# Routed expert rows: scaled when they leave PSUM, read back once at the end, added by VectorE and GpSimd

## The reference, cut to what matters

```python
h = modulate(rmsnorm(x, norm2), sh2, sc2)
x = x + g2 * hier_moe(h, ...)

def hier_moe(h, ...):
    # top-1 of 4 groups, then the top-2 of its 8 experts: two (expert, weight) pairs a token
    combine = ...                       # (tokens, groups, experts), two entries a token
    for g in range(4):
        a = einsum('td,edf->tef', t, w1[g]); b = einsum('td,edf->tef', t, w3[g])
        hid = silu(a) * b * combine[:, g, :, None]
        out = out + einsum('tef,efd->td', hid, w2[g])
```

## Time and profile before

| | |
|---|---|
| Median of 3 runs | 665.71 us (665.36 to 668.84) |
| The profiled execution | 666.92 us |
| Its span, first to last instruction | 665.1 us |
| TensorE matmul busy | 604.8 us, 91% of the span |
| VectorE busy | 304.1 us, 46% |
| GpSimd busy | 93.7 us, 14% |
| Moved from and to HBM | 165.36 MB read, 15.74 MB written |
| Mean granted TensorE clock | 0.973 of full speed |

### The profile page before, as it was taken

The page is one execution under the profiler, slowest core; times in us unless marked ns, Lnnn a source line. Parts: engine busy times, 40 slices in busy tenths (PEclk is TensorE's granted clock), DMA queues, the critical chain, the costliest instruction groups (busy, mean ns, idle before and its releaser), DMA issues.

```text
span 665.1 us, 7868 instructions
## 1 busy us (share of the span) xinstructions
PE 604.8 (91%) x3008; PEld 361.3 (54%) x3008; DVE 304.1 (46%) x606; ACT 168.9 (25%) x368; POOL 93.7 (14%) x136
## 2 busy tenths in 40 slices
PE   2699797889999999999999989999999987989785
PEld 0444585667767677774588834454444433434233
DVE  0229989375454444119525384332232322245167
ACT  3024031034444425343202301232222211112010
POOL 2022241037600000000000020211111111100000
PEclk9999899879999999999999999999999998999899
DMA  8994945923180303051456674799999999999963
GB/s 313 398 356 176 337 146 181 378 99 126 61 320 1 127 1 127 1 191 61 183 242 272 214 312 150 299 410 422 419 421 419 420 419 419 423 418 422 387 260 127
DMA packets 41498, 173.85 MB, mean 261 GB/s; under 512 B 6268, under 2 KB 6332, under 8 KB 28660
## 3 DMA queue, kind: packets, MB, share of 16 engines
q1 hardware_dynamic: 34128, 159.40, 60.6%
q0 software_dynamic: 5744, 12.84, 5.4%
q10 hardware_dynamic: 1588, 1.10, 0.5%
HBM read 165.36 MB, written 15.74 MB: 272 GB/s over the span
## 4 chain that ended last, share of the span: by engine, by line
PE 62%; DMA 14%; DVE 8%; SPq 6%; issue 6%; POOL 3%; ACTq 1%; ACT 1%; DVEq 0%; POOLq 0%
PE bank L917 11%; PE bank L642 6%; PE bank L644 6%; PE bank L643 6%; PE bank L949 5%; DMA late<-in_w_dram 4%; DMA arena<-in_w_dram 4%; PE bank L732 4%; SPq L520 3%; POOL ss L1877 3%; DMA qkg<-in_k_norm_dram 2%; PE bank L822 2%; DMA late<-in_w_in_dram 2%; PE bank L932 2%; PE bank L823 2%
## 5 line engine op out<-in xcount | busy, mean ns | idle before, releaser
L917 PE MATMUL bank<-arena,hT 128*64 128x512 f32 x352 | 86.2, 631 | 8.5 <-DMA arena<-in_w_dram 7.5
L642 PE MATMUL bank<-hT_high,w_in_parts 128*128 128x512 f32 x160 | 67.0, 419 | 3.3 <-DVE w_in_parts L1330 3.3
L644 PE MATMUL bank<-hT_high,w_in_parts 128*128 128x512 f32 x160 | 63.7, 398 | 0.0
L643 PE MATMUL bank<-hT_low,w_in_parts 128*128 128x512 f32 x160 | 63.6, 398 | 0.0
L917 PEld LDWEIGHTS bank<-arena,hT 128*64 128x64 f32 x352 | 24.5, 142 | 50.0 <-issue 40.9
L1199 ACT COPY probs<-bank 128x512 f32<-128x512 f32 x32 | 18.7, 586 | 121.3 <-PE bank L917 121.3
L1606 DVE TENSOR_SCALAR hT<-bank,ab 128x128 f32<-128x128 f32 x64 | 21.8, 403 | 50.1 <-PE bank L902 50.1
L917 PE MATMUL bank<-late,hT 128*64 128x512 f32 x160 | 39.0, 632 | 3.6 <-DMA late<-in_w_dram 3.6
L949 PE MATMUL bank<-arena,g1b 128*64 128x512 f32 x176 | 39.7, 593 | 2.2 <-DVE g1b L1621 2.2
L932 PEld LDWEIGHTS bank<-fold,probs 128*128 128x128 f32 x256 | 32.7, 197 | 16.0 <-issue 11.4
L1364 DVE TENSOR_REDUCE st<-bank 128x2 f32<-128x256 f32 (+3 forms) x16 | 13.2, 824 | 57.9 <-PE bank L668 57.8
(11 more groups left out here) (285 smaller groups left out, 1007.0 us busy)
## 6 DMA issues: line engine op xcount, KB each, us to landing
arena<-in_w_dram SPq DMA_DIRECT2D x66, 1024.0 KB, 23.0
late<-in_w_dram SPq DMA_DIRECT2D x30, 1024.0 KB, 24.2
late<-in_w_ada_dram SPq DMA_DIRECT2D x6, 2048.0 KB, 12.7
arena<-in_w_ada_dram SPq DMA_DIRECT2D x5, 2048.0 KB, 9.6
arena<-in_w_in_dram SPq DMA_DIRECT2D x4, 2048.0 KB, 16.8
late<-in_w_in_dram SPq DMA_DIRECT2D x4, 2048.0 KB, 11.2
y_scratch<-route POOLq DMA_DIRECT2D x1, 4096.0 KB, 14.9
late<-in_w_out_dram SPq DMA_DIRECT2D x2, 2048.0 KB, 7.6
```

The costliest lines, as they stand in the source:

```text
L642: mm(bank[:, b, :], wH[:, b, k, :], hH[:, k, :], start=k == 0, stop=False)
L643: mm(bank[:, b, :], wH[:, b, k, :], hL[:, k, :], start=False, stop=False)
L644: last = mm(bank[:, b, :], wL[:, b, k, :], hH[:, k, :], start=False, stop=k == 7)
L917: last = mm(bank[r, 2 + n % 2, :].rearrange("p (w f) -> p w f", w=2), xgT[n // 2 % 2][:, k, SLOTS * (n % 2):SLOTS * (n % 2 + 1)], w13[s][: ...
```

## The change

It does five things.

1. The weights of all 32 experts are spread to slots, not those of the last four. `combine_weights` runs before `one_hot(1, ...)`, on `[128, 4 x 32]` instead of `[128, 4 x 4]`. `weight_sums` gives all sixteen pairs four matmuls each: pairs 0 and 1 between the warming matmuls after `slot_sums(0)`, the others inside expert 1's gate_up.
2. Every `drain_y` multiplies by the slot's weight (a scalar per partition) as well as by `g2b`.
3. The stored rows are then added without a weight: `tensor_tensor` add, tiles 0 and 1 on VectorE (`BY_DVE = 2`), tiles 2 and 3 on GpSimd, each first for j = 0 and then for j = 1. VectorE's first two adds come after `hidden(31)`, its other two after the low parts of the last pair. All wait for all four readback DMAs, on one semaphore.
4. The readback waits, besides the scatters, for the landing of the last expert's w2. The ring loads go w1/w3 of e + 1 and e + 2, then w2 of e and e + 1.
5. Two warming matmuls of 256 columns stand ahead of gate_up(30), ahead of gate_up(31) and after it, and the one-hot spreading matrix is built at expert 29 instead of 31.

```diff
+BY_DVE = 2
...
             def load_pair(e):
-                for j in range(2):
-                    sp.wait_ge(ab_done, e + j + 1 - RING)
-                    load13(e + j, (e + j) % RING)
+                for n in range(e + 1, min(e + 3, E)):
+                    sp.wait_ge(ab_done, n + 1 - RING)
+                    load13(n, n % RING)
                 sp.wait_ge(y_done, e // 2 + 1 - RING // 2)
-                for j in range(2):
-                    load2(e + j, (e + j) % RING)
+                for n in range(e, e + 2):
+                    load2(n, n % RING)
...
-            sp.wait_ge(ab_done, 2)
-            load13(RING + 1, 1)
-            sp.wait_ge(y_done, 1)
-            load2(RING, 0)
-            load2(RING + 1, 1)
-            for e in range(RING + 2, E, 2):
+            for e in range(RING, E, 2):
                 load_pair(e)
...
             for i in range(3):
                 sp.wait_ge(y_stored[i], 16 * len(range(i, STORED, 3)))
-            rows_of(y_d, yg_loaded)
+            sp.wait_ge(w2_loaded[(E - 1) % RING], 16 * ((E - 1) // RING + 1))
+            for t in range(TT):
+                sp.dma_start(yg[:, t], y_d[2 * P * t:2 * P * (t + 1), :].rearrange("(p j) d -> p j d", j=2)
+                             ).then_inc(yg_loaded, 16)
...
+            def weight_sums(g, q):
+                e = 2 * (q - IDX_GROUPS[g][0])
+                for t in range(TT):
+                    lhs = place[g][t][:, e:e + 2, :].rearrange("p e s -> p (e s)")
+                    last = mm(bank[:, 7, W0 + 6 * q:W0 + 6 * q + 6], lhs,
+                              cparts[:, t, 2 * q:2 * q + 2, :].rearrange("p e c -> p (e c)"),
+                              start=t == 0, stop=t == TT - 1)
+                return last
...
             slot_sums(0)
-            keep_warm(7, 5)
+            keep_warm(5, 5)
+            pe.wait_ge(weights_ready, 1)
+            for q in IDX_GROUPS[0]:
+                weight_sums(0, q)
+            keep_warm(2, 5)
...
                     fold_halves(n - 1)
+                if n >= E - 2:
+                    keep_warm(2, 0, 0, CH // 2)
                 gate_up(n)
                 if n % 2 == 0 and n >= 2:
                     down(n - 2)
+                if n == E - 1:
+                    keep_warm(2, 0, 0, CH // 2)
...
-                    last = v.tensor_tensor(ysb[q % 3][:, w], bank[:, 6 + h, :], g2b[:, w], ALU.mult)
+                    last = v.scalar_tensor_tensor(out=ysb[q % 3][:, w], in0=bank[:, 6 + h, :], scalar=cws[:, q:q + 1],
+                                                  in1=g2b[:, w], op0=ALU.mult, op1=ALU.mult)
...
-                dve.wait_ge(yg_loaded[0], 16)
-                add_stored(0)
-                dve.wait_ge(yg_loaded[1], 16)
-                add_stored(1)
...
-            for t in range(2, TT):
-                dve.wait_ge(yg_loaded[t], 16)
-                add_stored(t)
+            def add_row(t, j):
+                v.tensor_tensor(xs[:, t, :], yg[:, t, j, :], xs[:, t, :], ALU.add).then_inc(x_added, 1)
+                dve.wait_ge(x_added, BY_DVE * j + t + 1)
+
+            dve.wait_ge(yg_loaded, 16 * TT)
+            add_row(0, 0)
+            add_row(1, 0)
             drain_last(1)
             for h in range(2):
                 y_low(1, h)
+            add_row(0, 1)
+            add_row(1, 1)
             for n in range(2 * TT):
                 t, w = n % TT, slice(CH * (n // TT), CH * (n // TT + 1))
                 dve.wait_ge(spread_done, n + 1)
+                if t >= BY_DVE:
+                    dve.wait_ge(rows_added, 2 * (TT - BY_DVE))
                 v.tensor_tensor(xs[:, t, w], bank[:, n, :], xs[:, t, w], ALU.add).then_inc(out_ready, 1)
...
+            pool.wait_ge(yg_loaded, 16 * TT)
+            for j in range(2):
+                for t in range(BY_DVE, TT):
+                    n = TT - BY_DVE
+                    if j == 1:
+                        pool.wait_ge(rows_added, n)
+                    g.tensor_tensor(xs[:, t, :], yg[:, t, j, :], xs[:, t, :], ALU.add).then_inc(rows_added, 1)
```

More of the change, by code:

```diff
@@ L374, in hybrid_trunk @@
         y_stored = [sem(f"y_stored{i}") for i in range(3)]
-        yg_loaded = [sem(f"yg_loaded{i}") for i in range(TT)]
         y_zeroed = sem("y_zeroed")
+        weights_ready = sem("weights_ready")
+        yg_loaded = sem("yg_loaded")
+        rows_added = sem("rows_added")
         zeros_ready = sem("zeros_ready")
@@ L567, in overflow @@
                 sp.sem_inc(x_turns, 1)
-            def rows_of(table, done):
-                for t in range(TT):
-                    sp.dma_start(yg[:, t], table[2 * P * t:2 * P * (t + 1), :].rearrange("(p j) d -> p j d", j=2)
-                                 ).then_inc(done[t], 16)
             def overflow_zeros():
@@ L879, in slot_sums @@
                                       start=t == 0, stop=t == TT - 1)
-                    if q >= STORED:
-                        i = q - STORED
-                        for t in range(TT):
-                            e = 2 * (q - IDX_GROUPS[g][0])
-                            lhs = place[g][t][:, e:e + 2, :].rearrange("p e s -> p (e s)")
-                            last = mm(idx_bank(g)[:, 64 + 6 * i:64 + 6 * i + 6], lhs,
-                                      cparts[:, t, 2 * i:2 * i + 2, :].rearrange("p e c -> p (e c)"),
-                                      start=t == 0, stop=t == TT - 1)
+                    if g == 1:
+                        last = weight_sums(g, q)
                 if q == IDX_GROUPS[g][-1]:
                     last.then_inc(idx_psum, 1)
+            def weight_sums(g, q):
[6 more added lines that the diff above has]
+                return last
             keep_warm(2, 5)
             slot_sums(0)
-            keep_warm(7, 5)
+            keep_warm(5, 5)
[3 more added lines that the diff above has]
+            keep_warm(2, 5)
             def gather_transposes(q):
@@ L1596, in _ @@
             indices(0)
+            combine_weights()
             one_hot(1, range(0, 2))
@@ L1641, in drain_last @@
                     w = slice(CH * h, CH * (h + 1))
-                    last = v.scalar_tensor_tensor(out=ysb[q % 3][:, w], in0=bank[:, 6 + h, :], scalar=cws[:, i:i + 1],
+                    last = v.scalar_tensor_tensor(out=ysb[q % 3][:, w], in0=bank[:, 6 + h, :], scalar=cws[:, q:q + 1],
                                                   in1=g2b[:, w], op0=ALU.mult, op1=ALU.mult)
@@ L1655, in y_low, with add_overflow_rows @@
                     last.then_inc(yL_ready, 1)
-            def add_stored(t):
+            def add_overflow_rows(t):
+                dve.wait_ge(y2_loaded, 16 * TT)
                 for j in range(2):
```

63 lines of the change are left out of this document (32 added, 31 removed).

## The result

| | before | after |
|---|---|---|
| Median | 665.75 us (665.36 to 668.84, 4 runs) | 674.33 us (672.21 to 675.19, 4 runs) |
| Ratio to before | | 1.0114, 95% interval 1.008 to 1.0148 |
| Profiled execution: time and span | 666.92, 665.1 us | 675.17, 673.4 us |
| Mean granted TensorE clock | 0.973 | 0.964 |

The change makes the kernel slower by 1.1%; the forecast was 673.0 us. In the two profiles the span grew by 8.3 us.

What follows compares the result with a forecast made beforehand. Bound: a saturated expert-weight stream from about 427 us, then the readback-and-add tail. Stream -2.2 us, first add at 648.0 for 642.1, single-file adds to 664.2, span 672.4 against 665.1: +7.3, so 673.0 us; range 665.0 to 677.0.

Steps and rivals of the forecast that it cites:

- The start of the stream: Expert weight loads near 427 us: saturation starts 2.2 us earlier, at 425.0, with bounds of 3.5 and 0.5 us.
- slow patch: TensorE near the stream's start: four gate_up matmuls take 1.89 instead of about 0.95 us; may lengthen by 1.7 us.
- slower, through the stream: Rival: 48 matmuls lengthen TensorE's slow patch, stream starts only 0.5 us earlier, time 674.7 us; chance 0.12.
- The end of the stream and the readback: Last w2 lands at 635.6, then four readbacks take 12.4 us (bounds 10 and 14); all rows in at 648.0.
- slower HBM: Readback: at the skill's 358 GB/s, 4.19 MB take 11.7 instead of 10.0 us, making the sum 1.7 us later.
- Single file: Tail: VectorE's and GpSimd's adds and low parts exclude each other, 5.2 + 1.4 + 9.6 = 16.2 us, to 664.2.
- The halves: Output adds after the file: eight halves take 4.9 us, less 0.6 for halves possibly already out, charged 4.3.
- the end, 3.9: Kernel's end: the span ends 3.9 us after the last output half, as before.
- What costs nothing: Expert weights block 0 to 0.2 us; freed TensorE work, down(30) ending near 642, worth nothing because the readback lands later.
- the readback's 7.3 us: Readback issue: SyncE now waits for the last w2's landing; before, it issued 7.3 us earlier, behind the weights.
- side by side: Rival in the tail: the exclusion does not bite, both engines add in parallel, time 666.2 us, no change; chance 0.25.
- Faster: Rival: earlier stream and freed TensorE reach the end, rows in before 645, no add waits, 661.8 us; chance 0.08.

Runs made afterwards that it cites:

- e3: Kernel before with only the change's new order of ring loads: 663.50 us, ratio 0.9952 to before.
- e9: Kernel before with weights by slot for all pairs, scaled drains and plain adds, all on VectorE, old load order: 666.89 us, ratio 1.0013.
- e5: Changed kernel with all row adds on VectorE and the readback not waiting for the last w2: 669.56 us, ratio 1.0057 to before.
- e6: As e5, but each token tile has its own semaphore and is added when it lands: 660.24 us, ratio 0.9912 to before.
- e1: Changed kernel with all eight row adds on VectorE, none on GpSimd: 672.13 us, ratio 1.0084 to before.
- e4: Changed kernel with the old order of ring loads: 677.09 us, ratio 1.0163 to before.
- e8: Changed kernel with GpSimd's four adds left out, so its output is incomplete: 669.07 us, ratio 1.0036 to before.
- e10: As e6, but tiles 2 and 3 added by GpSimd again: 663.99 us, ratio 0.9966 to before.
- e7: Kernel before, weighted adds kept on VectorE, plus new load order, warming matmuls, early spreading matrix, adds by tile after hidden(31): 660.66 us, ratio 0.9928.
- e2: Changed kernel with the readback waiting only for the scatters, not the last w2: 670.06 us, ratio 1.0071 to before.
- e6b: The e6 kernel unchanged, measured again on the same chip as e10: 663.10 us, ratio 0.9954 to before.

## Why the prediction was right, step by step

The forecast, 673.0 us and slower by over 0.5%, came from its own mechanism: a late readback and adds in single file. But every term of the sum was off: three were 3.3 us too small together and two 2.4 too large. That the span came out within 1.0 us is luck in part. Against the changed kernel's profile:

| step | forecast | profile |
|---|---|---|
| last w2 in, readback issued | 635.6 | 637.24 |
| issue to all rows in | 12.4 | 13.5 |
| file of adds and low parts | 16.2, to 664.2 | 14.6, to 665.4 |
| halves behind the file | 4.3 | 4.9 |
| end behind the last half | 3.9 | 3.1 |
| span | 672.4 | 673.4 |

- **The start of the stream, -2.2 us.** The term is 3.5 us won by the order less 1.3 lost by the sums by slot. The order held: with it alone (e3) expert 8's w1 is issued 3.6 us earlier and the kernel is 3.2 us faster. The sums cost 1.0, as shown under e9. But the prediction carried TensorE's slow patch of 414 to 416 over into the changed kernel: gate_up(0) to gate_up(2) takes 17.33 us before and 16.02 in e3, and the patch was a stretch of lower granted clock and no property of the place, as 410 to 418 show, first before, then after:

```profile
410.00:418.00 8.00, 8.00 (x113) 4.71 (x110) 2.55 (x14) 0.58 (x1) 0.98 (x1) 0.79 0.68 257
```

```profile
410.00:418.00 8.00, 8.00 (x184) 5.26 (x185) 0.23 (x2) 0.28 (x1) 0.00 (x0) 1.00 0.63 256
```

So the load at 425.45, close to the forecast 425.0, is luck: this profile has no patch there, but 2.0 us of half clock in front; e5 and e6, with neither, have that load at 422.50 and 423.18. The rival "slower, through the stream" (0.12) was built on the patch and falls in this profile.

- **The end of the stream and the readback, 12.4 us.** The last w2 was in at 637.24, 0.6 us ahead of the 637.8 that the prediction worked out for before, though the stream had started 1.7 earlier: the step that takes the start's gain over to the end in full did not hold. With the start 0.5 us late this makes the 1.6 us of the first row; where the 1.1 us between went isn't shown. The four reads then took 13.5, within the bounds of 10 and 14 and nearly the same in e1, e4 and e8 (13.4 to 13.7). The price of 12.4 came from four weight loads of one shape on quiet queues. What made the table's reads 1.1 us longer wasn't tried. And the 1.7 us that the prediction adds for a slower HBM belong to its lower bound of 10 us, not to the sum, which takes its 12.4 from a row.
- **Single file, 16.2 us.** The mechanism held: in e1 and e8 the cost goes with GpSimd's adds, and in both profiles the adds' lengths add up. The length was 1.6 us too much. VectorE's adds were priced at 1.31 us, that of the weighted ones, and plain ones take 1.22: 0.4 of the 1.6. The rest is GpSimd's. Its add of 1024 columns was taken at 2.4 us; the shortest here is 2.34 (e10, its last one, beside an idle VectorE), so the price was right for an add alone, but in the file it costs less: 14.6 us, less four adds of 1.22 and two low parts of 0.65, leave 2.1 for each of GpSimd's four. Why, no run shows. The Trainium skill ("GPSIMD Engine Reference", section 3.1) has 4497 ns for 2048 columns, 2.25 us as an estimate for half of it, between the two measured values.
- **The halves, 4.3 us, and the end, 3.9.** I had let two halves out before the last GpSimd add. VectorE's own last add came last in the file, so none was. The end behind the last half took 3.1 us, in e1, e6 and e8 too; what it is made of wasn't tried.
- **What costs nothing.** This held: `down(30)` ended at 644.2 (forecast about 642; e5, without the half clock in front, has 640.9), gate_up(0) waited 0.37 us for VectorE (forecast 0 to 0.2), and VectorE idled 11.07 us before its first add (forecast 8 or more). In e7 the same freed work, put under a readback that comes early, is part of a gain of 0.7%: worth nothing was a statement on this order of waits, as it said.
- **What the forecast did not separate.** It put the late first add down to the readback's 7.3 us. The runs show that issuing early brings only 2.9 (e2), and 3.8 with VectorE alone (e5), and that joining four landings on one semaphore costs 7 to 10 us (e5 against the two readings of e6; e2 against e10). The sum had counted this, since it let everything start when the fourth tile was in, but it gave the blame to the wait for w2.

The rival "side by side" (0.25) falls with e1 and e8. "Faster" (0.08) needed rows in by 645; even where they were in by 645.5 (e2), the rest kept the time above before's.

## What to carry to other kernels

Where data come back in pieces, consume each piece behind its own semaphore: work that overlaps the landing of the next piece is free, and one semaphore for all of them puts the whole of it behind the last. Before moving element-wise work with two SBUF operands from VectorE to GpSimd, look in the trace for a place where both run such operations at once; if their lengths add up there, the second engine is a slower place in the same queue; in these runs only work that reads one operand from PSUM ran beside it. And a stretch in which a few TensorE instructions take twice their time should be compared with its granted clock before it enters a sum, since the next execution may have it elsewhere.

## What the runs showed of the hardware that I had not expected

- **The turns are strict.** In the changed kernel's profile VectorE's and GpSimd's two-input operations alternate one for one until GpSimd's are done, 12.2 us; neither engine gets two in a row while the other has one ready. The Trainium skill ("SBUF — State Buffer", section on two separate sides) describes the exclusive hold and says that the one which starts first has it for its whole instruction; the drains and halves with an operand in PSUM, which were not held (1.41 us for two drains, 1.87 us for three halves in e10), agree with its condition of two SBUF inputs.
- **Half clock in a busy stretch.** TensorE was granted 0.57 between 381 and 389 us in one kernel and 1.00 in the other, with the same matmuls in both, and in both it had been busy at 1.00 for the 6 us before. In e6b that stretch stood at 0.79 and the one from 410 to 424 at 0.76, and the stream's start, the issue of expert 8's w1, slid to 427.27 us from the 423.18 of e6's profile, which has 1.00 in both stretches. The kernel is the same; 4.1 us is what such stretches did to one execution here.
